# The normed x written into the output, and the output tiles added to it by the DMA

## The reference

```
# end of the first block
x = x + g2[:, None, :] * ffn
return rms_norm(x, final_norm_g)                       # the "normed x"

# second block, on that x
h = rms_norm_2(x, g_pre) * (1 + scale) + shift
... projections, a forgetting attention and a sliding-window attention, both gated ...
y = jnp.concatenate([oa, ob], axis=-1) @ w_out         # 1024 x 1024 by 1024 x 1024
x = x + gate[:, None, :] * rms_norm_2(y, g_post)       # the output
```

## Time and profile before

| | |
|---|---|
| median of 3 runs | 2132.12 us (2131.53 to 2133.43) |
| profiled execution, its own time | 2129.92 us |
| its span, first to last instruction | 2128.1 us |
| TensorE, matmuls | 2036.1 us busy, 96% |
| VectorE | 1108.1 us busy, 52% |
| ScalarE | 871.5 us busy, 41% |
| GpSimd | 61.5 us busy, 3% |
| moved by DMA | 217.12 MB, mean 102 GB/s |
| granted TensorE clock, mean | 0.988 of full speed |

### The profile page before, as it was taken

One profiled execution on the slowest core, in us unless ns is written; L12 is line 12 of the kernel. 1 busy time (PEld: TensorE's weight loads), 2 busy tenths in 40 slices (PEclk: granted clock), 3 DMA queues, 4 the chain that ended last, 5 costly groups with the idle time before them and its releaser, 6 DMA issues.

```text
span 2128.1 us, 23716 instructions
## 1 busy us (share of the span) xinstructions
PE 2036.1 (96%) x9232; PEld 1583.3 (74%) x9232; DVE 1108.1 (52%) x1534; ACT 871.5 (41%) x1315; POOL 61.5 (3%) x115
## 2 busy tenths in 40 slices
PE   4999999999889899999999999999999999999897
PEld 2778876656777788888888888887877876776575
DVE  5685747555575655533355333346433454345645
ACT  4433345555443433332343333234414664355642
POOL 1001100000000000000000000000010000000000
PEclk8999999999999999999999999999999999999998
DMA  8335410010204545533333223333331000003043
GB/s 337 99 119 198 158 40 10 1 50 1 90 1 148 186 151 190 186 99 120 123 104 139 96 93 103 124 121 137 110 122 65 30 32 29 20 30 129 1 168 119
DMA packets 63198, 217.12 MB, mean 102 GB/s; under 512 B 6640, under 2 KB 7792, under 8 KB 62832
## 3 DMA queue, kind: packets, MB, share of 16 engines
q1 hardware_dynamic: 48944, 161.07, 22.4%
q0 software_dynamic: 14144, 54.53, 7.4%
HBM read 187.79 MB, written 25.17 MB: 100 GB/s over the span
## 4 chain that ended last, share of the span: by engine, by line
PE 84%; DVE 7%; ACT 4%; DMA 2%; issue 2%; SPq 1%; POOL 0%; DVEq 0%; ACTq 0%
PE ps L932 21%; PE ps L934 20%; PE ps L933 20%; PE ps L1066 9%; PE ps L1042 3%; PE ps L1043 2%; PE ps L1009 2%; DMA w_raw<-in_weights 2%; PE ps L1024 1%; DMA cmask<-in_consts 1%; SPq L2235 1%; DVE w_lo L1686 1%; ACT w_hi L1286 1%; PE ps L1012 1%; DVE slot L1682 1%
## 5 line engine op out<-in xcount | busy, mean ns | idle before, releaser
L932 PE MATMUL ps<-h_hi,w_hi 128*128 128x512 f32 x1504 | 600.2, 399 | 21.6 <-DVE h_lo L1719 10.1
L934 PE MATMUL ps<-h_hi,w_lo 128*128 128x512 f32 x1504 | 590.2, 392 | 0.0
L933 PE MATMUL ps<-h_lo,w_hi 128*128 128x512 f32 x1504 | 589.7, 392 | 0.0
L1686 DVE TENSOR_TENSOR w_lo<-w_raw,w_hi 128x1024 fp32r<-128x1024 f32 x222 | 271.8, 1225 | 493.2 <-ACT w_hi L1286 492.1
L1286 ACT ACTIVATE w_hi<-w_raw 128x1024 fp32r<-128x1024 f32 x222 | 234.7, 1057 | 523.6 <-DMA w_raw<-in_weights 521.9
L932 PEld LDWEIGHTS ps<-h_hi,w_hi 128*128 128x128 f32 x1504 | 285.4, 190 | 86.7 <-issue 21.5
L934 PEld LDWEIGHTS ps<-h_hi,w_lo 128*128 128x128 f32 x1504 | 284.6, 189 | 60.8
L933 PEld LDWEIGHTS ps<-h_lo,w_hi 128*128 128x128 f32 x1504 | 285.1, 190 | 58.6 <-issue 1.9
L1810 DVE TENSOR_REDUCE mh<-ps 128x1 f32<-128x512 f32 x192 | 124.7, 654 | 147.4 <-PE ps L1009 70.4
L932 PE MATMUL ps<-hid_hi,w_hi 128*128 128x512 f32 x352 | 136.9, 389 | 0.0
L933 PE MATMUL ps<-hid_lo,w_hi 128*128 128x512 f32 x352 | 136.9, 389 | 0.0
(11 more groups left out here) (305 smaller groups left out, 2616.0 us busy)
## 6 DMA issues: line engine op xcount, KB each, us to landing
w_raw<-in_weights SPq DMA_DIRECT2D x222, 512.0 KB, 3.5
ada_next<-in_ada POOLq DMA_DIRECT2D x32, 512.0 KB, 4.7
ada_last<-in_ada POOLq DMA_DIRECT2D x24, 512.0 KB, 4.3
ada_first<-in_ada SPq DMA_DIRECT2D x8, 1024.0 KB, 14.9
m_scratch<-y POOLq DMA_DIRECT2D x12, 512.0 KB, 4.9
xt<-in_x SPq DMA_DIRECT2D x2, 2048.0 KB, 16.8
y<-m_scratch SPq DMA_DIRECT2D x4, 1024.0 KB, 6.2
x_again<-in_x SPq DMA_DIRECT2D x16, 256.0 KB, 3.7
```

The lines of the kernel that those rows point to most:

```text
L932: e.matmul(o, w_hi[slot][:, tile_of(kw)], hi, start=start, stop=False)
L933: e.matmul(o, w_hi[slot][:, tile_of(kw)], lo, start=False, stop=False)
L934: return e.matmul(o, w_lo[slot][:, tile_of(kw)], hi, start=False, stop=stop)
L1686: return e.tensor_tensor(dst, src, hi.bitcast(F32), ALU.subtract)
```

## The change

The scratch `xb_scratch` is gone. GpSimd writes each half of the normed x into the output tensor itself, at the place where the output will be. The eight reloads into `xb`, and SyncE's waits that stood ahead of them, are gone, and so are VectorE's sixteen additions. All eight DMAs of the output are issued by GpSimd, each when its two tiles have been multiplied and both writes of the normed x have landed, and they carry `accum_op=ALU.add`: the DMA adds the tiles to what lies in the output. The program's end waits for the two writes as well as for the outputs.

```
@@ VectorE, y_tile(n, k)
-                i, t = 8 * n + k + 1, yo[:, n, k, :]
+                t = yo[:, n, k, :]
                 e.wait_ge(s["norm_r"], norm_no("yr", n))
                 tt(t, t, rs3[n][:, :], ALU.mult).then_inc(s["y3_n"], 1)
-                e.wait_ge(s["y3_n"], i)
-                e.wait_ge(s[f"xb_in{n}"], 64)
-                tt(t, t, xb[:, n, k, :], ALU.add).then_inc(s["y3_add"], 1)
@@ GpSimd, final_normed(n, k)
                 if k == KT - 1:
                     e.wait_ge(s["x_scaled"], no("ft", n, k))
-                    e.dma_start(xb_dram[n], x2[:, :, :]).then_inc(s["xb_kept"], 16)
+                    e.dma_start(out[:, :, half_of(n)].rearrange("k p t -> p k t"), x2[:, :, :]).then_inc(s["xb_kept"], 16)
@@ GpSimd, y_tile(n, k)
-                if n == 0 and k % 2:
-                    e.wait_ge(s["y3_add"], k + 1)
-                    e.dma_start(out[k - 1:k + 1, :, half_of(n)].rearrange("k p t -> p k t"), yo[:, n, k - 1:k + 1, :]).then_inc(s[f"out{n}"], 16)
+                if k % 2:
+                    e.wait_ge(s["y3_n"], 8 * n + k + 1)
+                    e.wait_ge(s["xb_kept"], 32)
+                    e.dma_start(out[k - 1:k + 1, :, half_of(n)].rearrange("k p t -> p k t"), yo[:, n, k - 1:k + 1, :],
+                                accum_op=ALU.add).then_inc(s[f"out{n}"], 16)
@@ SyncE
-            def wout2(n, j):
-                if n == 0:
-                    half, k0 = j // 4, 2 * (j % 4)
-                    e.wait_ge(s["mix2_lo"], KT)
-                    e.wait_ge(s["val"], no("val", "fox", 7, 1, KT - 1))
-                    e.wait_ge(s["xb_kept"], 32)
-                    e.dma_start(xb[:, half, k0:k0 + 2, :], xb_dram[half][:, k0:k0 + 2, :]).then_inc(s[f"xb_in{half}"], 16)
-            def y_tile(n, k):
-                if n and k % 2:
-                    e.wait_ge(s["y3_add"], 8 * n + k + 1)
-                    e.dma_start(out[k - 1:k + 1, :, half_of(n)].rearrange("k p t -> p k t"), yo[:, n, k - 1:k + 1, :]).then_inc(s[f"out{n}"], 16)
             def end():
+                e.wait_ge(s["xb_kept"], 32)
                 for n in range(2):
                     e.wait_ge(s[f"out{n}"], 64)
```

More of the change, by code:

```diff
@@ L93 @@
     "y2_out fsel_in pos_in swap_in z_kept ob_kept ob_in sz_in fz_in fg_act fg_vec fg_tr cols_made cum_hi cum_lo ang sines fsel_made rope2 "
-    "gate2 mix2_hi mix2_lo post_made xb_in0 xb_in1 y3_out y3_n y3_add out0 out1 ").split()
+    "gate2 mix2_hi mix2_lo post_made y3_out y3_n out0 out1 ").split()
 class Plan:
@@ L713, in build @@
         x1_dram = nc.dram_tensor("x1_scratch", (2, KT, P, HT), F32, kind="Internal").ap()
-        xb_dram = nc.dram_tensor("xb_scratch", (2, P, KT, HT), F32, kind="Internal").ap()
         z_dram = nc.dram_tensor("z_scratch", (8, P, T), F32, kind="Internal").ap()
@@ L2331, in sync @@
                     "gate": gate, "wout": wout, "down": down, "angle": angle, "swap": swap,
-                    "reload": reload, "wout2": wout2, "yt": y_tile, "end": end}
+                    "reload": reload, "end": end}
             for kind, *which in plan.steps:
```

## The result

Over 22 runs of each kernel the changed one takes 2135.6 us, the one before 2131.77 us (medians). The ratio is 1.0019, 95% interval 1.0012 to 1.0026: about 4.0 us slower (2.6 to 5.5 us by the interval). So there is a change, though it is just under the 0.2% (4.3 us) that the prediction took as the least that can be told. 2134.0 us was forecast, in a range of 2127.1 to 2142.0.

The account below looks back on a forecast made before the run. TensorE, busy for 96% of the span, was taken as the bound, leaving mainly the tail to matter. -5.75 (additions) + 7.95 (queue, second reads, later start) - 0.3 (second write) = +1.9 us, so 2134.0 us, range 2127.1 to 2142.0.

Parts of the forecast that it names:

- The additions: Tail behind TensorE's last matmul: removing VectorE's eight second-half additions saves 5.75 us, all on the path.
- The queue and the accumulation: Tail: queued transfers, second reads and a later start of the second half's outputs cost +7.95 us.
- x: Time of one accumulating 512 KB output, taken as 3.10 us: an output's 1.37 us plus a load's 1.73 us.
- my marker: First-half accumulating output, 3.1 us before, should land in about 4.8 us; under 3.3 or over 5.4 us means wrong.
- The form 2117.09 + 4x + 0.40: Tail's end: first byte at 2117.09 us, four queued accumulations, 0.40 us from last byte to semaphore; 2129.89 us.
- The move to GpSimd: Second half's four outputs leave SyncE's queue: issue 0.73 to 0.90 us, bytes moving 1.30 us after issue.
- The first half: First half's outputs in the last projection: accumulating under busy TensorE, with eight additions off VectorE, changes 0 us.
- the reload: Last projection: removing eight 512 KB loads of 4.3 us each from SyncE's queue is worth 0.
- The second write: Second write of the normed x, mid-kernel: 2 KB pieces let a weight load through sooner, removing TensorE's 0.34 us wait; -0.3 us.
- The cheap accumulation: Rival for the tail: accumulating costs the same as a plain output, 1.37 us; change -5.0 us, 2127.1 us; chance 13%.
- The latency case: Rival for the tail: fetching the destination holds up the write, up to 6.6 us each; change up to +14.2 us; chance 34%.
- The forecast case: Tail: accumulation runs at two reads, 3.10 us each; 2134.0 us, no change that can be told; chance 53%.

Follow-up runs that it names:

- Experiment 2: Kernel before without VectorE's eight second-half additions, outputs plain from SyncE, so that half lacks the normed x; ratio 0.9978, 4.7 us faster.
- experiment 1: Kernel before, with the second half's four plain outputs issued by GpSimd instead of SyncE, additions still on VectorE; ratio 1.0014, 3.0 us slower.
- experiment 3: Changed kernel with plain instead of accumulating outputs in the second half, still from GpSimd, so that half lacks the normed x; ratio 0.9993 to the kernel before.
- experiment 8: Kernel before, plus one small GpSimd memset of an unread tile after the last addition; ratio 1.0037.
- experiment 4: Kernel before, with the change made for the first half only and the second half left as it was; ratio 1.0002.
- experiment 6: Kernel before, second half: two multiplications then two additions, but the first pair accumulates on GpSimd and three go out on SyncE; ratio 0.9997 to the kernel before.
- experiment 7: Kernel before, but in the second half GpSimd adds the even tiles and VectorE the odd; outputs plain from SyncE; ratio 1.0025, slower.
- experiment 5: Kernel before, with VectorE's second-half order changed to two multiplications, then their two additions; ratio 0.9993.
- experiment 9: Kernel before, second half: two multiplications then two additions, and the last pair sent on SyncE as two 256 KB pieces; ratio 0.9989, 2.3 us faster.

## Why the prediction was right, and where it was not

**The additions** were booked at 5.75 us less on VectorE. Experiment 2 measures 4.7 us at the end, since plain outputs queue without them, which the sum had in its other term. Right.

**The queue and the accumulation** were booked at +7.95 us, a wait for the outputs that ends 2127.7 + 2.2 us on the old clock, 15.7 us after the first multiplication. It ended after 15.6 us. But this agreement is luck: two errors cancel. x was put at 3.10 us, by adding a load's engine time to an output's. As engine time that is nearly right (2.9 us), but packets overlap, and the pace of the queue, which is what the sum needs, is 2.57 us. By the Trainium skill's ratio of 1.93 (Collectives: The Full Stack, "The bandwidth ceiling: the fold count and why AG ≠ RS ≠ AR") x would be an estimated 2.64 us, and the trace agrees better with that than with my sum: 2.57 us is 1.88 times 1.37 us, and 1.81 times the 1.42 us of 369 GB/s. Whether two reads on one ring are the reason was not tried. Against the shorter x stands a later start: from the first pair's issue to full rate the changed kernel needs some 4 us (15 GB/s up to 2123 us, 131 up to 2125), where the plain output needs 1.30. A first-half accumulation, with none queued ahead of it, lands after 6.4 us; my marker was 4.8 us, and over 5.4 us I was to be wrong. So by its own sign the prediction is wrong here, in the form of this term: x is 1.2 us above the plain output, and some 2 us more are fixed, 0.46 of them in the issue (1.19 for 0.73 us). What the rest of the fixed time is, no run shows. The form 2117.09 + 4x + 0.40 lacks this constant. 4 x 2.57 + 5.3 us gives the same 15.6 us as 4 x 3.10 + 3.3 us.

**The move to GpSimd** was priced by its first byte and its issue, and the only wait considered at the end was SyncE's. The step that failed is "its wait for the outputs ends at 2127.7 us ... is the number to beat": the span ends when all engines have drained, and GpSimd's drain, hidden before at 2106.1 us, became the last. That is +2.2 us, in no term of the sum, and about the difference between the +1.9 us forecast and the 4.0 measured. Experiments 1 and 3 show it without accumulation, experiment 8 without DMA. The four pieces add up: additions -4.7 (experiment 2), GpSimd's later landing +0.6 (9.4 - 8.8, experiments 3 and 2), accumulation +6.2 (15.6 - 9.4), end +2.2 (2.6 for 0.4): +4.3 us in the trace.

**The first half** and **the reload** were booked at 0: ratio 1.0002 in experiment 4, and TensorE is busy for 40.00 of 40.00 us (2069 to 2109 us) beside the accumulations in the changed kernel as well. Right, for half of the reload; the other half is gone only in kernels that changed the tail.

**The second write** was booked at -0.3 us. The wait of 0.34 us is absent in both kernels that write 2 KB pieces there (the changed one and experiment 3), and stands, with 0.3 to 1.4 us, in the nine others. ScalarE's wait for the weight behind that write is 6.9 and 7.0 us in the two and 8.1 us or more where the second write goes to the scratch, as forecast. Right, and too small to time.

**The rivals.** The cheap accumulation is out (2.57 against 1.37 us). The latency case, x above 3.69 us, is out as a rate, though some 2 us of fixed time at the start stand in the trace, which may be that latency, paid once; no run shows it. The forecast case's own range, 2127.9 to 2136.4 us, holds the 2135.6 us, near its upper end: the case was "no change that can be told", and the 22 runs of each kernel did tell one, slower by 2.6 to 5.5 us. The whole range was 15 us wide, and would have held a much faster kernel as well.

What GpSimd's drain follows stays partly open. With outputs in flight it ended 2.2 to 2.4 us after their last landing, five times (the changed kernel, experiments 1, 3, 4 and 6). With nothing of GpSimd's own in flight it ended 7.8 us after its last instruction, twice (experiments 7 and 8). But in the kernel before, and as much in experiments 2, 5 and 9, it ended 7.8 us after its last issue was done, 5.4 us after the landing, and in experiment 1 only 4.8 us after its last issue was done. No single rule that I know covers all of them.

## What to carry to other kernels

A DMA that adds is a slower transfer: here 2.57 us for 512 KB where a plain one takes 1.37, and 2 us more before it runs. Use it where the transfer is covered, as in the first half (where it cost nothing that can be told, and gained nothing), not behind the last computation, where the engine's addition (0.6 us for 256 KB) was cheaper. And look at who finishes last, not only at who lands last: give an engine with a long drain no work near the end. What paid in the tail was small and local: an order without back-to-back dependences (1.0 us in the trace), and a smaller last piece (0.2 us).

## What the runs showed of the hardware that I had not expected

- GpSimd's drain at the end of the program takes 5.5 to 12.8 us from the start of its last instruction, and a memset of 0.10 us exposed 5.0 us of it.
- An accumulating DMA of 512 KB takes GpSimd 1.19 us to issue, a plain one 0.73.
- Beside one accumulation, plain outputs on another queue land in 5.5 us (median of three) instead of 2.9.
- VectorE's and GpSimd's additions, each with both inputs in SBUF, run at 1.63 and 1.64 us together; VectorE's alone takes 0.69.
- A dependence between neighbouring VectorE instructions costs 0.11 to 0.12 us (0.72 to 0.73 for 0.61 us from start to start), 1.0 us over the sixteen.
